# Four edits to the order of work in a two-block model on one core: first loads in quarters, a value product by k tile, key sums behind a projection, last squares added in PSUM

## What is computed

```python
def reference(x, norm_g, w_out, e_w_in, ...):
    x = first_block(x, ...)            # 2 layers
    return second_block(x, ...)        # 1 layer, then the final norm

# first_block, layer 0: h = rmsnorm(x); u_val, u_gate, z_a, q, k, v, z = h @ e_w_in
#   y_a = conformer_conv(u_val, u_gate) * silu(z_a); y_b = moba(norm(q), norm(k), v) * silu(z)
# first_block, layer 1: h = rmsnorm(x)
#   (q_c, kc, vc, ks, vs, kw, vw, g_c, z_c, q_d, k_d, v_d, z_d) = split(h @ o_w_in)
#   sparse attention over the compressed (kc, vc), selected (ks, vs) and window (kw, vw) keys,
#   with gates sigmoid(g_c); banded attention over norm(q_d), norm(k_d), v_d
# both layers: x = x + concat(y1, y2) @ w_out
# second_block: retention and dilated attention, then x + g2 * (square(relu(h @ w1)) @ w2)
#   and at the end rms_norm(x, norm_f_g)
```

## Time and profile before

| | us |
| --- | --- |
| median of 3 runs | 909.28 |
| lowest, highest | 907.03, 910.65 |
| the profiled execution, device time | 910.96 |
| its span | 909.2 |
| PE busy | 882.9 (97%) |
| POOL, ACT, DVE busy | 609.0, 446.7, 428.8 |

### The profile page before, as it was taken

One profiled execution on the slowest core, in us unless ns is written; L12 is line 12 of the kernel. 1 busy time (PEld: TensorE's weight loads), 2 busy tenths in 40 slices (PEclk: granted clock), 3 DMA queues, 4 the chain that ended last, 5 costly groups with the idle time before them and its releaser, 6 DMA issues.

```text
span 909.2 us, 16515 instructions
## 1 busy us (share of the span) xinstructions
PE 882.9 (97%) x6792; PEld 826.0 (91%) x6792; DVE 428.8 (47%) x952; ACT 446.7 (49%) x665; POOL 609.0 (67%) x485
## 2 busy tenths in 40 slices
PE   6999999899999999999999999999999999999997
PEld 5898889897777999888988799999999999999996
DVE  3998665743875466882445232331124562211001
ACT  3434667344555453354444547586334775533330
POOL 0766468740000669989777777768889999997880
PEclk9999999999999999999999999999999999999999
DMA  9844577783210279597666444444536655545421
GB/s 347 344 146 158 214 243 266 252 307 131 100 48 1 93 275 391 219 376 261 226 213 232 149 176 145 154 167 156 216 139 232 231 185 187 185 141 186 185 94 47
DMA packets 27907, 177.61 MB, mean 195 GB/s; under 512 B 3080, under 2 KB 5780, under 8 KB 7480
## 3 DMA queue, kind: packets, MB, share of 16 engines
q1 hardware_dynamic: 26248, 174.35, 53.1%
q10 hardware_dynamic: 1584, 2.20, 0.7%
HBM read 174.95 MB, written 3.43 MB: 196 GB/s over the span
## 4 chain that ended last, share of the span: by engine, by line
PE 90%; DVE 4%; ACT 2%; issue 1%; DMA 1%; POOL 1%; ACTq 0%; DVEq 0%; SPq 0%
PE proj L742 18%; PE proj L744 18%; PE proj L745 18%; PE proj L717 5%; PE proj L822 3%; PE proj L819 3%; PE proj L821 3%; PE proj L1016 3%; PE proj L778 2%; PE mixed L968 1%; PE proj L1089 1%; PE transposed L937 1%; PE scores L923 1%; PE mixed L951 1%; PE sums L876 1%
## 5 line engine op out<-in xcount | busy, mean ns | idle before, releaser
L656 POOL TENSOR_TENSOR w_lo<-raw,w_hi 128x512 fp32r<-128x512 f32 x328 | 418.9, 1313 | 208.2 <-ACT w_hi L1374 208.1
L744 PE MATMUL proj<-parts,w_lo 128*128 128x256 f32 x952 | 266.4, 280 | 0.6 <-POOL w_lo L656 0.6
L742 PE MATMUL proj<-parts,w_hi 128*128 128x256 f32 x904 | 257.3, 285 | 0.5 <-POOL w_lo L656 0.3
L745 PE MATMUL proj<-parts,w_hi 128*128 128x256 f32 x904 | 252.6, 279 | 0.0
L1374 ACT ACTIVATE w_hi<-raw 128x2048 fp32r<-128x2048 f32 x82 | 156.8, 1914 | 112.4 <-DMA raw<-in_weights 61.0
L744 PEld LDWEIGHTS proj<-parts,w_lo 128*128 128x128 f32 x952 | 179.1, 188 | 1.7 <-POOL w_lo L656 0.8
L742 PEld LDWEIGHTS proj<-parts,w_hi 128*128 128x128 f32 x904 | 169.9, 188 | 2.8 <-issue 2.1
L745 PEld LDWEIGHTS proj<-parts,w_hi 128*128 128x128 f32 x904 | 170.4, 188 | 0.0
L656 POOL TENSOR_TENSOR w_lo<-arena,w_hi 128x512 fp32r<-128x512 f32 (+2 forms) x44 | 56.2, 1317 | 56.5 <-ACT w_hi L1374 56.5
L742 PE MATMUL proj<-hid_hi,w_hi 128*128 128x256 f32 x160 | 45.3, 283 | 0.0
L819 PE MATMUL proj<-w_hi,parts 128*128 128x512 f32 x112 | 45.0, 402 | 0.0
(11 more groups left out here) (402 smaller groups left out, 2111.7 us busy)
## 6 DMA issues: line engine op xcount, KB each, us to landing
raw<-in_weights SPq DMA_DIRECT2D x105, 1024.0 KB, 5.0
arena<-in_weights SPq DMA_DIRECT2D x32, 1024.0 KB, 7.2
wide<-in_weights SPq DMA_DIRECT2D x9, 1024.0 KB, 7.0
probT<-in_weights SPq DMA_DIRECT2D x8, 1024.0 KB, 5.6
dil_lines<-dil_line SPq DMA_DIRECT2D x1, 2304.0 KB, 12.9
prob<-in_weights SPq DMA_DIRECT2D x2, 1024.0 KB, 4.9
dil_bias<-dil_lines SPq DMA_DIRECT2D x1, 1536.0 KB, 9.4
xT<-in_x SPq DMA_DIRECT2D x2, 512.0 KB, 5.8
```

Source lines behind the costliest of these rows:

```text
L656: nc.gpsimd.tensor_tensor(lo_slots[RAW_AT[n]][:, at], raw_slots[RAW_AT[n]][:, at], hi_slots[HI_AT[m]][:, at].bitcast(F32), ALU.subtract).t ...
L742: nc.tensor.matmul(dst, whi, h, start=first, stop=False)
L744: nc.tensor.matmul(dst, wlo, h, start=False, stop=False)
L745: last = nc.tensor.matmul(dst, whi, lo[:, k, :], start=False, stop=stop)
```

## The change

Four places change.

The start: x and `uv0` come in four pieces of 256 KB each, with a semaphore for each piece, instead of two of 512 KB. `first_unit` waits for a piece of the unit every second k tile.

`vsvw`: `split_tokens` runs its k tiles outermost where it stands behind a fresh norm, so that the matmuls of both token halves follow each `h_ready`. `vdgt` keeps its order.

The key norm: the sums of `kskw` go behind `qc0`, and the spreads `sp_ks` and `sp_kw` behind `qc1`.

The last norm: the square of k tile 0 is written by ACT into PSUM, DVE adds those of tiles 1 to 6 there, the total goes to `wide`, and PE sums the total and the last tile's squares behind `f2_7`. The spread is done twice, into `st` and into `sc[0]`; ACT copies the second one to SBUF and POOL scales the last of the four output pieces with it. SP issues two of the four stores, ACT the other two.

```diff
     out += own([f"wo0_{i}" for i in range(4)])
-    out += own(["kcvc", "kskw", "vsvw", "qc0"]) + [("sp_ks", []), ("sp_kw", [])] + own(["qc1", "vdgt"])
+    out += own(["kcvc", "kskw", "vsvw", "qc0", "qc1"]) + [("sp_ks", []), ("sp_kw", [])] + own(["vdgt"])
     out += [("hidk", ["ck0", "ck1"]), ("qd0", ["qd0"]), ("hTk", []), ("hidv", ["cv0", "cv1"]), ("kc2", []), ("hTv", [])]
...
         def _(sp):
-            for i, half_in in enumerate((sem("uv0_half"), raw_in[RAW_AT[0]])):
-                at = slice(UNIT // 2 * i, UNIT // 2 * (i + 1))
-                sp.dma_start(xT[:, 4 * i:4 * i + 4], cut(a["x"], S)[:, 4 * i:4 * i + 4]).then_inc(x_in[i], 16)
-                sp.dma_start(raw_slots[RAW_AT[0]][:, at], a["weights"][0][:, at]).then_inc(half_in, 16)
+            for i in range(4):
+                at = slice(UNIT // 4 * i, UNIT // 4 * (i + 1))
+                sp.dma_start(xT[:, 2 * i:2 * i + 2], cut(a["x"], S)[:, 2 * i:2 * i + 2]).then_inc(x_in[i], 16)
+                sp.dma_start(raw_slots[RAW_AT[0]][:, at], a["weights"][0][:, at]).then_inc(first_unit_in[i], 16)
             for u in LOADS[1:]:
...
                     sp.dma_start(dil_bias[:].rearrange("p g h j -> p (g h) j"), skew).then_inc(sem("dil_in"), 16)
+            for i in (0, 2):
+                sp.wait_ge(sem("scaled"), i + 1)
+                sp.dma_start(out[:, 512 * i:512 * i + 512], wide[:, 512 * i:512 * i + 512]).then_inc(sem("stored"), 16)
+            sp.wait_ge(sem("stored"), 64)
...
+            pool.wait_ge(sem("x_gained"), KD)
+            pool.wait_ge(sem("last_rstd"), 1)
+            nc.gpsimd.tensor_tensor(cut(wide[:, 1536:2048], S), h32[:, 6:8], rstd[:, 0:S].unsqueeze(1).broadcast_to([P, 2, S]), ALU.mult) \
+                .then_inc(sem("scaled_pool"), 1)
...
                 whi, wlo = weight(name)
-                for t in range(TT):
-                    for k in range(KD):
-                        if t == 0 and fresh is not None:
-                            pe.wait_ge(h_ready, KD * fresh + k + 1)
-                        at, dst = slice(P * t, P * t + P), b[:, S * t:S * t + n]
-                        nc.tensor.matmul(dst, parts[:, 0, k, at], whi[:, k, 0:n], start=k == 0, stop=False)
-                        second_half(name, k)
-                        nc.tensor.matmul(dst, parts[:, 0, k, at], wlo[:, k, 0:n], start=False, stop=False)
-                        last = nc.tensor.matmul(dst, parts[:, 1, k, at], whi[:, k, 0:n], start=False, stop=k == KD - 1)
+                todo = [(k, t) for t in range(TT) for k in range(KD)] if fresh is None else [(k, t) for k in range(KD) for t in range(TT)]
+                for k, t in todo:
+                    if t == 0 and fresh is not None:
+                        pe.wait_ge(h_ready, KD * fresh + k + 1)
+                    at, dst = slice(P * t, P * t + P), b[:, S * t:S * t + n]
+                    first = k == 0 and (t == 0 or fresh is None)
+                    nc.tensor.matmul(dst, parts[:, 0, k, at], whi[:, k, 0:n], start=first, stop=False)
+                    second_half(name, k)
+                    nc.tensor.matmul(dst, parts[:, 0, k, at], wlo[:, k, 0:n], start=False, stop=False)
+                    last = nc.tensor.matmul(dst, parts[:, 1, k, at], whi[:, k, 0:n], start=False,
+                                            stop=k == KD - 1 and (t == TT - 1 or fresh is None))
                 end(last)
...
-            def stream_spread(name):
+            def stream_spread(name, to=st, done=None):
...
                 for t in range(TT):
-                    last = nc.tensor.matmul(st[:, S + P * t:S + P * t + P], stream_rstd[:, 2 * t:2 * t + 1].broadcast_to([P, P]), ident,
+                    last = nc.tensor.matmul(to[:, S + P * t:S + P * t + P], stream_rstd[:, 2 * t:2 * t + 1].broadcast_to([P, P]), ident,
                                             start=True, stop=True)
-                last.then_inc(sem("stream_spread"), 1)
+                last.then_inc(done or sem("stream_spread"), 1)
...
                 w = cut(raw_slots[RAW_AT[0]], 256)
-                pe.wait_ge(sem("uv0_half"), 16)
                 for k in range(KD):
                     pe.wait_ge(sem("x_scaled"), k + 1)
-                    if k == KD // 2:
-                        pe.wait_ge(raw_in[RAW_AT[0]], raw_target(0))
+                    if k % 2 == 0:
+                        pe.wait_ge(first_unit_in[k // 2], 16)
                     for j in range(2):
...
             split_tokens("vsvw", 2 * P, 1)
+            project("qc0")
             head_sums("kskw")
-            project("qc0")
+            project("qc1")
             spread("sp_ks", 0, 1, "kskw")
             spread("sp_kw", 1, 1, "kskw")
-            project("qc1")
             head_sums("qc0")
...
                 features(f"f2_{i}", hid_hi, hid_lo, [[(f"f2_{i}a", 0, 0), (f"f2_{i}b", 0, 16)]], wait)
-                if i and i % 2 == 0:
-                    stream_sums("xf", i // 2 - 1)
-            stream_sums("xf", 3)
+                if i == KD - 1:
+                    pe.wait_ge(norm_done, NORM_AT["xf"])
+                    pe.wait_ge(sem("sq_total"), len(BEFORE_NORM) + 1)
+                    column_sums(0, True, False)
+            pe.wait_ge(stream_sq, squares_of("xf", KD - 1))
+            column_sums(KD - 1, False, True).then_inc(norm_sum, 1)
+            state["norm"] += 1
             stream_spread("xf")
+            stream_spread("xf", sc[0], sem("second_spread"))
             assert state["filled"] == len(BANKED) and state["norm"] == len(NORMS)
...
             for i in range(4):
-                stream_squares(2 * i, 2 * i + 2, (x_in[i // 2], 16))
+                stream_squares(2 * i, 2 * i + 2, (x_in[i], 16))
...
                 passing(f"f2_{i}")
-                stream_squares(i, i + 1, f"f2_{i}")
+                if i == 0:
+                    act.wait_ge(*evacuated("f2_0"))
+                    act.wait_ge(norm_done, NORM_AT["xf"])
+                    nc.scalar.activation(st[:, S:2 * S], xT[:, 0, :], ACT.Square).then_inc(stream_sq, 1)
+                else:
+                    stream_squares(i, i + 1, f"f2_{i}")
                 if i < KD - 1:
...
             gained(KD - 1)
-            for i in range(4):
-                act.wait_ge(h_full, KD * 3 + i + 1)
+            act.wait_ge(sem("second_spread"), 1)
+            nc.scalar.activation(rstd[:, 0:S], sc[0][:, S:2 * S], ACT.Copy).then_inc(sem("last_rstd"), 1)
+            for i in (1, 3):
+                act.wait_ge(sem("scaled") if i == 1 else sem("scaled_pool"), 2 if i == 1 else 1)
                 act.dma_start(out[:, 512 * i:512 * i + 512], wide[:, 512 * i:512 * i + 512]).then_inc(sem("stored"), 16)
...
                 if name == "xf":
-                    for i in range(4):
+                    for i in range(3):
                         dve.wait_ge(sem("x_gained"), 2 * i + 2)
                         V.tensor_tensor(cut(wide[:, 512 * i:512 * i + 512], S), h32[:, 2 * i:2 * i + 2],
-                                        spread.unsqueeze(1).broadcast_to([P, 2, S]), ALU.mult).then_inc(h_full, 1)
+                                        spread.unsqueeze(1).broadcast_to([P, 2, S]), ALU.mult).then_inc(sem("scaled"), 1)
                     return
...
             for k in range(KD):
-                dve.wait_ge(x_in[k // 4], 16)
+                dve.wait_ge(x_in[k // 2], 16)
                 V.tensor_scalar(x_scaled[:, k, :], xT[:, k, :], col("norm_g", k), None, ALU.mult).then_inc(sem("x_scaled"), 1)
...
                 gated(xT[:, k, :], ready(f"f2_{k}")[:, 0:S], k, 40).then_inc(free_of(f"f2_{k}"), 1)
-                if k % 2:
-                    fold_squares("xf", k // 2)
+                if 0 < k < KD - 1:
+                    dve.wait_ge(stream_sq, squares_of("xf", k))
+                    ins = V.tensor_tensor(wide[:, 0:S] if k == KD - 2 else st[:, S:2 * S], wide[:, S * k:S * k + S], st[:, S:2 * S], ALU.add)
+                    if k == KD - 2:
+                        ins.then_inc(sem("sq_total"), 1)
+                    else:
+                        own.did(ins)
+                        own.settle()
             stream_norm("xf", None)
```

More of the change, by code:

```diff
@@ L485, in mixer_kernel @@
         first_in, setup_in = sem("first_in"), sem("setup_in")
-        x_in = [sem("x_in0"), sem("x_in1")]
+        x_in = [sem(f"x_in{i}") for i in range(4)]
+        first_unit_in = [sem(f"uv0_in{i}") for i in range(3)] + [raw_in[RAW_AT[0]]]
         const_in, rot_in = sem("const_in"), sem("rot_in")
```

## The result

| | us, median | lowest, highest | runs |
| --- | --- | --- | --- |
| before | 909.58 | 906.77, 911.38 | 21 |
| changed | 914.05 | 909.08, 917.74 | 21 |

The ratio is 1.0048, with a 95% interval of 1.0033 to 1.0063. The forecast was 907.1, with 904.2 to 909.8 as its range: it missed the size and the sign. The profiled execution of the changed kernel took 912.93, with a span of 911.1.

What follows compares the result with a forecast made beforehand. PE was taken as the bound, 90% of the chain that ended last. Start -0.7, value product and key norm 0, end -1.5 sum to -2.2: 907.1 us against the median of 909.28, range 904.2 to 909.8.

Steps and rivals of the forecast that it cites:

- the new wait ahead of vdgt: Odd layer: PE stands 1.25 us, 181.0 to 182.3, until ACT has squared and copied qc1 out of vdgt's bank.
- both edits of the odd layer together give 0: Value product and moved key sums: PE's 1.2 us lead at vdgt is lost waiting for ACT by kc2.
- besides: In the late-load case, PE's standing might bring a third half-clock stretch of 3.4 us, costing up to 1.7 more: 911.3.
- the signs of being wrong: Prediction wrong if half-clock stretches come or go elsewhere, or if qd1's load is issued at another time.
- Start: First loads in 256 KB pieces: they land 0.9 us sooner, of which 0.7 is kept.
- my bound of 1.6: Start: most that PE's first product could gain, 7.42 less DVE's first scaled tile at 5.85.
- so the gain carries on: After the start PE has no wait for a load until the odd layer, keeping the start's gain.
- Value product and key norm: Odd layer: 0.75 us at the value product and the 1.5 us key-norm wait removed, but 0 in the sum.
- The balance of 0 at kc2: Odd layer: kc2 starts at 200.7, before 200.67; bounds 1.2 gained or 1.5 lost, by qd1's landing.
- End: Last norm: 1.5 us gained, 1.3 from three sums between f2's products and 0.2 from the last store.
- all gained: Rival, chance 0.2: qd1 lands early or ACT's order doesn't bind; up to 5.3 us gained, 904.0 to 905.5.
- Slower: Rival, chance 0.1: qd1 lands late, each us beyond 192.6 lost at kc2; 909.6 with another turn of 2.5 us.

Runs made afterwards that it cites:

- The run with the wait alone: Kernel before, with one added wait of PE ahead of vdgt until ACT has copied qc1: 915.52 us against 909.5, ratio 1.0074.
- the run with the wait filled: Changed kernel with ten added matmuls, result unread, in PE's wait ahead of vdgt: 908.7 us, ratio 0.9997 against the kernel before.
- both waits taken away and the start's wait filled: Changed kernel, qc0's sums ahead of the spreads, qd1's high part behind hidk's copy, two unread matmuls at 39 us: 906.68 us against 909.94 before.
- the odd layer alone: Kernel before plus only the value product by k tile and the key sums behind qc0: 917.6 us, ratio 1.0085.
- the run with both waits taken away: Changed kernel with qc0's sums ahead of the spreads and qd1's high part on ACT behind hidk's copy: 907.97 us, ratio 0.9984 against before.
- the sums of qc0 first: Changed kernel with the sums of qc0 ahead of the two spreads instead of behind them: median 911.74 us, in two heaps.

## Why the prediction was wrong, by its own steps

**What failed** is one step: that the new wait ahead of vdgt costs its own 1.25 us and no more, with which "both edits of the odd layer together give 0". I had the half-clock stretches in view and gave a further one 1.7 us, as a thing that might happen "besides" in the case of a late load. I also named half-clock stretches among the signs of being wrong, without a price in the range. They belonged to the forecast itself. The wait was foreseen, at its place and to 0.1 us; behind it PE got 1.2 GHz for 13.6 us, where I had at most 3.4 in view, and from vdgt to kc2 it took 6.4 us longer. The run with the wait alone shows the price, 6.0 us in the median, and the run with the wait filled shows the way back, 5.4.

**The sum, as forecast and as found.** Start: 0.7 was forecast; the first product moved by 1.8 (a load of 256 KB took 4.3 us where 512 KB took 6.2), so my bound of 1.6 was too low: the gain's columns landed sooner too, at 4.5. The sums behind the first unit came at 14.90 for 16.48, 1.6 ahead. The step "so the gain carries on" did not hold: PE then stood 0.5 us for DVE at 39 us, a wait that before doesn't have, and in the changed kernel's profile 1.0 of the 1.6 is left at 53 us (52.08 for 53.04). In the profiles of the start alone and of start and end, half clock follows this wait and PE is 0.5 to 1.0 behind before at the same sums. The median of the start alone kept 0.8. That this is near 0.7 is luck. The Trainium skill's rule of 1 MiB per DMA ("DMA: Bandwidth & Descriptors", "Rules for kernel authors") is about bandwidth; here the first landing counts, and quarters won.

**Value product and key norm**: both old waits went, qc1 stood 0.6 for POOL (0.4 forecast), qd1's load landed at 192.3 (192.6). The order of the steps up to vdgt holds, but the lead there was too high: PE enters the layer 0.9 ahead of before (sums at 151.59 for 152.50) and reaches vdgt 1.5 ahead, so the layer itself gives 0.6 where 1.2 was forecast. The rest is lost up to the end of qc1: the spreads begin at 178.64, and the forecast of 179.0 less the start's 0.9 is 178.1. The balance of 0 at kc2 fails: it is +4.9, or +5.9 with the 0.9 of the start. With the wait filled, hTk waits 0.8 for ACT, kc2 another 0.3, and kc2 starts at 201.9, 1.2 behind before. With both waits taken away and the start's wait filled it starts at 199.2, 0.7 better than PE's lead at the entry.

**End**: 1.5 forecast; in the profile of the end alone 1.4 in all. The sums gave all of it (1.3 forecast); the 0.2 of the stores is there at their issue and not in the end of the span. POOL's piece was not held up beside DVE: 1.27 us, where POOL's pieces of this size took 1.31 in the mean. So the trace agrees with what the Trainium skill, "SBUF — State Buffer" ("SBUF: two separate sides"), has for a DVE instruction with one SBUF input.

**Rivals**: "all gained" needed both new waits gone, and with them gone the time is 906.7 to 908.0, short of its 904 to 905.5. (Its terms were added wrongly: 2.5 + 1.6 + 1.5 is 5.6, and 1.2 + 1.6 + 1.5 is 4.3, so 903.7 to 905.0.) "Slower" named a late load as the way and needed 199.3 for 0.5%; the time came out at its size by another way.

**Left open.** Why 0.7 us ahead of vdgt brings 13.6 us of half clock while before's 1.5 ahead of the key sums brings none, and 1.9 there brings 6.8. The places differ in how light the work around them is, but no run varied that by itself. Nor do the parts add up: the odd layer alone cost 7.8 us in the median (917.6 against 909.77) and start and end gained 1.1, where all of it together cost 4.5. Runs of the changed kernel at 909.1 had a mean clock of 0.995 and those at 914 to 914.6 one of 0.986, so some executions probably escape the long stretch; only one has a profile. That 0.5 us for DVE at 39 us brought half clock in three profiles is open too: the changed kernel has the same wait of 0.52 without it, and the run with both waits taken away one of 1.1.

## What to carry to other kernels

A short wait of TensorE is not priced by its own length. Where a change adds one, even of 0.7 us, put a half-clock stretch behind it into the range (here 13.6 us of it, which cost half its length), and look at PEclk by windows before and after; the list of waits does not show it. Not every wait brings one, and these runs don't tell in advance which will. When PE is moved ahead of the engines that feed it, the next place where it stands has to be found too: here it was hTk, and at the start the product at 39 us. Ten matmuls whose result nobody reads, put into the wait, were worth 5 us (908.7 for 914.05); taking both waits away by order was worth at least as much (907.97), and these two are within each other's noise.

## What the runs showed of the hardware

Idle time of 0.7 us and of 1.3 us at the same place, ahead of vdgt, gave a half-clock stretch of the same length, 13.6 us, in the kernel before with an added wait. The changed kernel has 13.6 behind its 1.3 us too, but the odd layer alone has 17.0 behind the same wait. The stretch began between 0 us (the odd layer alone) and 2.4 us (the changed kernel) after PE had resumed. During it PE was 100% busy and the granted clock still stayed at 0.50.

Executions of one and the same kernel fall into heaps that differ in the mean granted clock. With the sums of qc0 first, four ran at 906.0 to 907.3 us with 0.996, and six at 912.5 to 913.1 with 0.990 to 0.992. The kernel before has them too, closer together: beside the last group of runs, four at 906.9 to 907.2 with 0.998, and none of the others below 909.2, with 0.996 or less.
